# First stage of a hybrid trunk layer: relative bias loaded and multiplied before the first transposes, first four token tiles normalised on ScalarE

## The reference, cut to what matters

```python
h = layer_norm(x, ln_in_g, ln_in_b)            # x: 1024 tokens x 1024 channels, float32
proj = h @ w_in                                # columns a_q, a_k, a_v, b_q, b_f, ..., gate
bias = rel_bias[t5_band_buckets()]             # 32 buckets x 8 heads -> bias of every head and distance
s = einsum(q, k) * HEAD_DIM ** -0.5 + bias     # attention A, windows of two chunks of 64
```

## Time and profile before

| | |
|---|---|
| median of 3 runs | 2163.17 us (2161.89 to 2163.58) |
| span of the profiled execution, first to last instruction | 2158.9 us |
| median less that span | 4.3 us |
| PE busy | 2069.2 us, 96% of the span |
| DVE, POOL, ACT busy | 1086.9, 703.4, 423.6 us (50%, 33%, 20%) |

### The profile page before, as it was taken

How to read it: one execution, slowest core, us unless ns; L and a number is a source line. 1 busy time by engine, 2 the same in 40 slices (tenths; PEclk the granted TensorE clock), 3 DMA queues, 4 the chain that set the end, 5 groups by cost and what they waited for, 6 DMA issues and landing times. The chain is left out here.

```text
span 2158.9 us, 23073 instructions
## 1 busy us (share of the span) xinstructions
PE 2069.2 (96%) x7129; PEld 1093.2 (51%) x7130; DVE 1086.9 (50%) x2963; ACT 423.6 (20%) x909; POOL 703.4 (33%) x612
## 2 busy tenths in 40 slices
PE   7999999999999999999999999899999999999990
PEld 6445887574644555554444554444444444444440
DVE  6121445549451222212224656776666666666647
ACT  2111333334321111112221221011111111111112
POOL 1752002212032221203351001455445545545533
PEclk9999999999999999999999999999999999999995
DMA  5421000012122121126335004799999999999964
GB/s 147 115 87 39 20 20 20 20 45 73 45 74 78 54 69 56 61 71 226 98 103 205 30 40 165 282 340 355 347 348 355 361 357 358 350 354 354 349 197 157
DMA packets 129902, 368.24 MB, mean 171 GB/s; under 512 B 34333, under 2 KB 66193, under 8 KB 104353
## 3 DMA queue, kind: packets, MB, share of 16 engines
q1 hardware_dynamic: 104224, 312.64, 38.8%
q0 software_dynamic: 23520, 54.61, 10.5%
q10 hardware_dynamic: 2080, 0.01, 0.1%
HBM read 318.37 MB, written 68.16 MB: 179 GB/s over the span
## 5 line engine op out<-in xcount | busy, mean ns | idle before, releaser
L2993 PE MATMUL banks<-arena 128*128 128x512 f32 x1056 | 471.2, 599 | 5.8 <-DVE arena L2986 3.5
L2972 POOL DMA_INDIRECT arena<-h_rows,index x268 | 276.7, 1033 | 155.6 <-issue 76.8
L2993 PEld LDWEIGHTS banks<-arena 128*128 128x128 f32 x1056 | 196.2, 191 | 230.2 <-issue 226.2
L1712 PE MATMUL banks<-arena 128*128 128x512 f32 x616 | 279.7, 596 | 0.4 <-ACT arena L329 0.4
L3009 PE MATMUL banks<-arena 128*128 128x512 f32 x528 | 237.6, 592 | 1.3 <-ACT arena L2808 0.8
L285 PE MATMUL banks<-arena 128*128 128x512 f32 x480 | 221.9, 600 | 3.3 <-PEq L108 3.0
L2986 DVE STREAM_TRANSPOSE arena<-arena 128x1024 f32<-128x1024 f32 x66 | 133.9, 2028 | 135.2 <-PE banks L2993 135.2
L2980 POOL DMA_INDIRECT sums<-arena,row_to x66 | 107.1, 1623 | 271.1 <-DMA sums<-arena,row_to 247.1
L1712 PEld LDWEIGHTS banks<-arena 128*128 128x128 f32 x616 | 110.5, 190 | 116.1 <-issue 115.1
L3009 PEld LDWEIGHTS banks<-arena 128*128 128x128 f32 x528 | 100.2, 190 | 127.0 <-issue 125.3
L2956 DVE TENSOR_SCALAR index<-row 32x1 uint32<-32x1 f32 x1072 | 155.4, 145 | 17.1
(11 more groups left out here) (392 smaller groups left out, 2384.6 us busy)
## 6 DMA issues: line engine op xcount, KB each, us to landing
arena<-in_w_exp_gate_dram SPq DMA_DIRECT2D x66, 1024.0 KB
arena<-in_w_exp_up_dram SPq DMA_DIRECT2D x66, 1024.0 KB
arena<-in_w_exp_down_dram SPq DMA_DIRECT2D x66, 1024.0 KB
arena<-in_w_in_dram SPq DMA_DIRECT2D x26, 1024.0 KB, 5.2
gates<-arena SPq DMA_DIRECT2D x60, 256.0 KB, 2.0
arena<-gates SPq DMA_DIRECT2D x60, 256.0 KB, 2.6
arena<-h_rows,index POOLq DMA_INDIRECT x268
arena<-in_x_dram SPq DMA_DIRECT2D x8, 512.0 KB, 6.0
```

The costliest lines, as they stand in the source:

```text
L1712: mm = pe.matmul(gate_bank(n, b), left[:, k, :], right[:, k, :], start=(alone and k == 0), stop=(k == 3), skip_group_check=True)
L2972: return pool.indirect_dma_start(w.x[k][:, 256 * q:256 * (q + 1)], None, rows, bass.IndirectOffsetOnAxis(ap=g.index[:, k, q:q + 1], axis=0 ...
L2993: mm = pe.matmul(g.bank[:, 2, :].rearrange("p (a f) -> p a f", a=2), xT[:, k, :], wgu[:, :, k, :], start=(k == 0), stop=(k == KT - 1))
```

## The change

Four things move, all in the first stage:

- The two tables of the relative bias are loaded by ACT's queue as the first DMAs of the kernel, instead of by SP after the x tiles. DVE widens the bias table as its first instruction.
- PE runs `bias_rows` before the first transposes, with four banks (2 to 5) instead of two, so it waits for no copy. ACT's four copies stand between the normalisings of the first tiles.
- Tiles 0 to 3 are normalised by ACT, as rstd * x + shift; DVE makes shift = -mean * rstd, a new small instruction for each tile.
- Pieces 4 to 7 of tile 0 are turned into banks 2 to 5, so each of these transposes waits for one copy of `bias_read`.

```diff
@@ SP: first-stage loads
             loads = [
-                (g.relb[:], g.ins["rel_bias"]), (g.onehot, g.ins["bucket_onehot"]),
                 (g.sinks[:], row(g.ins["a_sinks"][0]).to_broadcast([P, A_HEADS])),
...
-            sp.wait_ge(rel_stored, 16)
+            sp.wait_ge(rel_moved, 48)
@@ ACT
+            for dst, src in ((g.relb[:], "rel_bias"), (g.onehot, "bucket_onehot")):
+                act.dma_start(dst, g.ins[src], allow_slow_non_contiguous=True).then_inc(rel_moved, 16)
...
-            for i in range(4):
+            def normalize(m):
+                act.wait_ge(rstd_done, 2 * (m + 1))
+                act.activation(x[:, m, :], x[:, m, :], ACT.Identity, bias=shift[:, m:m + 1],
+                               scale=rstd[:, m:m + 1]).then_inc(x_normed, 1)
+
+            def bias_read(i):
+                act.wait_ge(rel_ready, i + 1)
+                act.activation(relval[:, 2 * i:2 * i + 2, :], bank[:, 2 + i, :].rearrange("p (h n) -> p h n", h=2),
+                               ACT.Copy, scale=8.0).then_inc(rel_read, 1)
+
+            deviation(0)
+            normalize(0)
+            for i in range(1, 4):
+                bias_read(i - 1)
                 deviation(i)
+                normalize(i)
+            bias_read(3)
@@ DVE
-                dve.wait_ge(rstd_done, i + 1)
+                dve.wait_ge(rstd_done, 2 * i + 1)
+                if i < 4:
+                    dve.scalar_tensor_tensor(out=shift[:, now], in0=mv[:, i, 0:1], scalar=-1.0, in1=rstd[:, now],
+                                             op0=ALU.mult, op1=ALU.mult).then_inc(rstd_done, 1)
+                    return
@@ PE
                     for k in range(KT):
+                        if m == 0 and k >= 4:
+                            pe.wait_ge(rel_read, k - 3)
                         mm = pe.transpose(turn_bank(0, k)[:, m * P:(m + 1) * P],
...
+            bias_rows()
             turn_tiles()
...
-            bias_rows()
             for u in range(4, g.rows_unit):
```

More of the change, by code:

```diff
@@ L375, in norm_in_and_project @@
         sem("xT_read0"), sem("xT_read1")]
-    zeroed, zero_pad, rel_wide, rel_ready, rel_read, rel_stored, bias_in, rows_turned, rows_read = map(sem, (
-        "zeroed", "zero_pad", "rel_wide", "rel_ready", "rel_read", "rel_stored", "bias_in", "rows_turned",
+    zeroed, zero_pad, rel_wide, rel_ready, rel_read, rel_moved, bias_in, rows_turned, rows_read = map(sem, (
+        "zeroed", "zero_pad", "rel_wide", "rel_ready", "rel_read", "rel_moved", "bias_in", "rows_turned",
         "rows_read"))
@@ L384, in norm_in_and_project @@
     h_row = [g.region(WK + 3584, D), g.region(YT0 + NT * D, D)]
+    shift = g.sb("shift0", [P, 4])
     h_made, h_kept = sem("h_made"), [sem("h_kept0"), sem("h_kept1")]
@@ L461, in _ @@
             sp.dma_start(skew.rearrange("(p n) -> p n", p=P),
-                         relval.rearrange("p a b -> p (a b)")).then_inc(rel_stored, 16)
-            sp.wait_ge(rel_stored, 16)
+                         relval.rearrange("p a b -> p (a b)")).then_inc(rel_moved, 16)
+            sp.wait_ge(rel_moved, 48)
             wide = A_HEADS * 256
@@ L590, in _ @@
             read_unit(g, act, 3, banks)
[L591 to L595, removed]
             act.wait_ge(lbd, 1)
@@ L646, in turned @@
                                       ALU.mult, ALU.add).then_inc(xT_read[1], 1)
+            dve.wait_ge(rel_moved, 32)
+            dve.tensor_copy(g.relwide, bcast(g.relb[:].unsqueeze(2), [32, A_HEADS, P])).then_inc(rel_wide, 1)
             statistics(0)
@@ L657, in _ @@
             dve.wait_ge(g.params, g.n_params)
-            dve.tensor_copy(g.relwide, bcast(g.relb[:].unsqueeze(2), [32, A_HEADS, P])).then_inc(rel_wide, 1)
             turned(1)
@@ L738, in bias_rows @@
                 for h in range(A_HEADS):
-                    if h >= 4 and h % 2 == 0:
-                        pe.wait_ge(rel_read, h // 2 - 1)
-                    mm = pe.matmul(bank[:, 4 + h // 2 % 2, (h % 2) * 256:(h % 2 + 1) * 256],
+                    mm = pe.matmul(bank[:, 2 + h // 2, (h % 2) * 256:(h % 2 + 1) * 256],
                                    g.relwide[:, h, :], g.onehot, start=True, stop=True)
```

## The result

The changed kernel takes 2170.03 us (median, 2167.34 to 2172.07), the kernel before 2162.70 in the runs beside it (2160.88 to 2165.75): ratio 1.0032, 95% interval 1.0022 to 1.0042. It is slower by 7.3 us, where +3.9 was forecast, and 2170.03 lies 0.2 above the upper end of the range.

The account below looks back on a forecast made before the run. PE was taken as the bound, its start set by others and its wait at block 1 by slot 3's chain. +5.1 at the start less 1.2 gave +3.9 on 2158.9, 2162.8, plus 4.3 to the median: 2167.1 us, range 2162.3 to 2169.8.

Parts of the forecast that it names:

- Early loads and the widening: At the start, loading the tables first and widening on DVE was taken to delay nothing, at worst 1.8 us.
- rival 4: At the start, the tables land late, behind x: +1.8 us on everything, +5.7 in all, 2168.9 us; chance 0.07.
- A round on ACT: First tiles: copy, square root, DVE's reciprocal and shift, and normalising take 2.25 us for each further tile.
- PE behind the fourth copy: 25 transposes wait for ACT's last bias copy, start at 17.9, mostly slow; first projection 5.1 us later, bounds 3.3 to 5.8.
- T: Start of PE's first projection in the kernel before, 17.84 us.
- What of the 5.7 us reaches the end: Of 5.7 us gained by moving the bias products, slot 3's chain at block 1 passes on 1.2, bounds 0 and 3.2.
- U': End of unit 3 on PE in the changed kernel, forecast 5.1 us later than the 42.68 before.
- rivals 3 and 4: New pauses at block 1 slow PE's clock (+6.1 us, chance 0.12); tables land late at the start (+5.7, 0.07).
- Slot 3 in time: At block 1, slot 3 comes in time for PE, so all 5.7 us count: -0.6 us, 2162.6; chance 0.16.
- PE never slow: At the start, bias products keep PE awake and transposes go at 0.11 us: +2.1 us, 2165.3; chance 0.08.
- New pauses cost clock: At block 1, a slow spell after PE's second pause costs 2.2 us: +6.1 in all, 2169.3; chance 0.12.
- Copies don't pile up: At the start, PE keeps its old start (+0.5 us) with all 5.7 us gained: 2158.0 us; chance 0.04.

Follow-up runs that it names:

- e4: Changed kernel, but SP stores the bias, reads it back shifted and loads the two rows before issuing slot 2; 2161.60 us, 0.9998 of the kernel before.
- e1: Changed kernel, but DVE normalises tiles 0 to 3 as before, with the bias still first; 2165.98 us, 1.0013 of the kernel before.
- e2: Changed kernel with all bias work back in its old place, ACT still normalising tiles 0 to 3; 2162.01 us, 0.9999 of the kernel before.
- e5: e4 plus 14 unused transposes on PE in two waits of tile 0's turning; 2158.10 us, 0.9977 of the kernel before.
- e7: Changed kernel, but SP waits until slot 2 has landed before issuing the bias store; 2168.59 us, 1.0027 of the kernel before.
- e8: e6 plus 48 unused identity transposes at the very start of PE's list; 2155.43 us, 0.9962 of the kernel before.
- e10: e6 plus 20 unused identity transposes at PE's start and three behind each bias product; 2156.66 us, 0.9973 of the kernel before.
- e6: Changed kernel with the edits of e1 and e4 together; 2158.27 us, 0.9975 of the kernel before.
- e9: e6 plus 16 unused identity transposes at the very start of PE's list; 2155.46 us, 0.9966 of the kernel before.

## Why the prediction came out as it did

- **What bounds the kernel.** Right: PE's start and the chain behind slot 3 were the two places, and e4 shows the second by itself. The wait of 1.1 us is PE's only one up to 110 us, which is as far as the earlier trace rows reach; later stages have longer ones, but they come after both places.
- **Early loads and the widening, 0 taken, up to 1.8 as the bound.** It cost 0.75. The one-hot table took 4.5 us to land; 3.5 were thought enough. This is rival 4 at less than half its size.
- **A round on ACT, 2.25.** Measured 2.24, a normalising 1.24 as worked out.
- **PE behind the fourth copy.** Restart at 18.51 (17.9 forecast; the late tables account for it), then 5.16 us to the first projection, 4.83 of them the 25 transposes and the rest the first odd copy, against 5.0: T + 5.8 for T + 5.1. That this is the forecast's own upper bound is chance: the bound took the transposes as slow throughout and the tables as in time. e1, e2 and e5 show the mechanism from three sides. What I had not seen is that PE would be the bound right behind it: with the copies out of the way (e1) 2.5 us stay, as bias products and nearly all transposes run slow.
- **What of the 5.7 us reaches the end, 1.2 taken with bounds of 0 and 3.2.** This is the mis-sized term: it measured -0.9. The step that failed says that the store lands between U' + 6.7 and U' + 7.7, because slot 2 ahead of it would take 2.7 us of the DMA engines. The store was done at U' + 9.7. The 2.7 go by 393 GB/s, a rate read from 48 to 50 us of the kernel before, where slot 2 had landed and only the store was under way. Slot 2 alone took 5.1 us from issue to landing there, the store 3.9; side by side in the changed kernel the two moved 252 GB/s from 50 to 53 us, 205 from 53 to 54 and 437 from 54 to 56. e7 shows nearly the same total with the two strictly in a row, U' + 9.2, so 5.1 + 3.9 would have been the estimate to take. The lower bound of 0 was therefore no bound. What makes the pair slow when it runs together was not tested.
- **Sum.** 5.7 and 0.9 make 6.6 for 3.9: 0.7 of the miss lies in the start, most of it the tables, and 2.1 in the store. The medians say 7.3; the other 0.7 arises behind the mark and is not explained. The forecast had 0.55 on no change and 0.40 on slower; it came out slower, and mostly by the forecast's own path, not by that of rivals 3 and 4, which carried half of the chance for slower.
- **Rivals.** Slot 3 in time: fell (4.96 us of waiting). PE never slow: fell, by the pace of the 25. New pauses cost clock: a slow spell followed the first pause and was swallowed, as the text on that rival allowed; it cost nothing, as PE would have waited for the join at 98.14 anyway. Copies don't pile up: fell.

## What to carry to other kernels

Before moving work off a bound engine, follow the next wait on that engine to its source: here a wait of 1.1 us marked a DMA chain that took a gain of 5.7 us whole, and the order of a few DMA issues was worth more than the whole change. SP works its list in order too: a store whose data is ready waits for whatever the DMA ahead of it in the list waits for, here 27 us (49.02 in the changed kernel, 21.87 in e4). A DMA rate read in a stretch with one store alone does not price a load, nor the two together. When a step is put between others in a list, look at who waits for the last of them and at what stands behind the waiter. Idle time at a kernel's start is worth less than it looks: in these kernels PE worked there at half pace, and the bias products took 7.16 us at the start for 3.96 in their old place.

## What the runs showed of the hardware

- TensorE's clock fell while or just after PE ran products with 32 of 128 rows, without a pause. In e8 PE was fast, the products began at 9.69, and the granted clock fell to 0.50 at 12.9; with three full-row transposes behind each product it did not fall (e10). In e2, with the products in their old place from 42.35, it fell at 45.4; in the kernel before it fell at 46.9, just behind them, and reads 0.50 in the earlier trace rows. Nor did 7.16 us of such products at the start lift the pace (e1, e6 and the changed kernel), where e8's full-row transposes did. The Trainium skill ("TensorE: Matmul & The Clock Gate", Part 1) ties the clock to how busy PE was; here a PE busy all the time lost it.
- Extra work whose result nobody uses made the kernel faster: 14 transposes, 2.0 us earlier at the first projection and 3.5 us less in the median, with intervals apart (e5 against e4).
- The moment at which the pace rises differs between kernels that start alike: about 6.1 us in e8, between 5 and 6 in e10, but only at about 18 in e9, whose transposes ended at 6.4.
- At the start of an execution the profile's granted clock reads 1.00 while the pace is half (16 bias parts in 7.16 us in the changed kernel, 3.96 in the kernel before; 7 transposes from 5 to 6 us of e8 and 12 from 7 to 8, both at 1.00). The pace tells it there, not the column.
- A load and a store of 1.05 MB each, issued 0.4 us apart on one queue, took as long as one after the other (9.5 and 9.0 us).
